# Sixteen expert blocks' first product computed during the key selection

## The reference, cut to what matters

```
q = (x @ w_q).reshape(tokens, 8 heads, 2, 128)
s1, s2 = q[:, :, 0] @ subkeys[0].T, q[:, :, 1] @ subkeys[1].T     # 128 keys each
v1, i1 = top_k(s1, 16); v2, i2 = top_k(s2, 16)
sc, pos = top_k(v1[..., :, None] + v2[..., None, :], 16)           # of 256 sums
eidx = i1 * 128 + i2 at pos                                        # 16384 experts
g = softmax(sc)
act = gelu(u_tab[eidx] . x)                                        # a dot product for each pick
out = sum over the 8 * 16 picks of g * act * v_tab[eidx]
```

## Time and profile before

| | us |
|---|---|
| median of 3 runs | 3969.11 |
| lowest, highest | 3940.86, 3989.34 |
| the profiled execution | 3945.24 |
| its span, first to last instruction | 3943.5 |

### The profile page before, as it was taken

One profiled execution on the slowest core, in us unless ns is written; L12 is line 12 of the kernel. 1 busy time (PEld: TensorE's weight loads), 2 busy tenths in 40 slices (PEclk: granted clock), 3 DMA queues, 4 the chain that ended last, 5 costly groups with the idle time before them and its releaser, 6 DMA issues. The chain is left out here.

```text
span 3943.5 us, 58724 instructions
## 1 busy us (share of the span) xinstructions
PE 3521.6 (89%) x19976; PEld 3186.6 (81%) x19996; DVE 3441.3 (87%) x7119; ACT 1494.6 (38%) x3188; POOL 1092.0 (28%) x1008
## 2 busy tenths in 40 slices
PE   4979989288999999999978999865799999999997
PEld 4957889277999999999977678864699999999996
DVE  8966759997999999999989565699799999999998
ACT  3322332283444334444333222314744344434433
POOL 0000123392333333333200001225633333333331
PEclk9978989599999999999988889887999999999998
DMA  6610110269999999999856001104699999999996
GB/s 243 234 60 24 54 45 23 81 207 352 414 407 401 402 401 402 405 400 400 338 183 221 23 1 54 66 1 160 218 387 411 404 402 396 410 402 403 404 403 245
DMA packets 199853, 1033.81 MB, mean 262 GB/s; under 512 B 18521, under 2 KB 70297, under 8 KB 95713
## 3 DMA queue, kind: packets, MB, share of 16 engines
q0 software_dynamic: 73728, 536.90, 33.4%
q1 hardware_dynamic: 125922, 494.56, 32.7%
HBM read 977.84 MB, written 53.56 MB: 262 GB/s over the span
## 5 line engine op out<-in xcount | busy, mean ns | idle before, releaser
L1592 POOL DMA_INDIRECT held_rows<-in_uv_rows,chosen x428 | 551.9, 1290 | 1489.2 <-DVE y L1911 1373.5
L1773 PE MATMUL ps<-hd_hi,u_hi 128*128 128x384 f32 x2048 | 701.0, 342 | 28.3 <-DVE a_lo L1890 18.5
L1773 PE MATMUL ps<-hd_hi,u_lo 128*128 128x384 f32 x2048 | 693.9, 339 | 0.0
L1773 PE MATMUL ps<-hd_lo,u_hi 128*128 128x384 f32 x2048 | 693.5, 339 | 0.0
L1911 DVE SCALAR_TENSOR_TENSOR y<-held_rows,shares_now,y 128x1024 f32<-128x1024 f32 x428 | 546.1, 1276 | 1.6 <-ACT shares_now L1830 1.6
L1901 DVE CUSTOM_DVE_ANT_0 held_rows<-held_rows,h2rows 128x1024 f32<-128x1024 f32 x428 | 520.2, 1215 | 0.4 <-DMA held_rows<-in_uv_rows,chosen 0.4
L1784 PE MATMUL ps<-v_hi,a_hi 128*128 128x512 f32 x1536 | 476.7, 392 | 0.0
L1784 PE MATMUL ps<-v_lo,a_hi 128*128 128x512 f32 x1536 | 472.8, 389 | 0.0
L1784 PE MATMUL ps<-v_hi,a_lo 128*128 128x512 f32 x1536 | 472.8, 389 | 0.0
L1815 ACT ACTIVATE v_hi<-v_raw 128x1024 fp32r<-128x1024 f32 x256 | 271.1, 1059 | 413.3 <-PE ps L1784 410.3
L1773 PEld LDWEIGHTS ps<-hd_hi,u_hi 128*128 128x128 f32 x2048 | 387.7, 189 | 39.0 <-DVE u_lo L1875 29.2
(11 more groups left out here) (308 smaller groups left out, 6926.5 us busy)
## 6 DMA issues: line engine op xcount, KB each, us to landing
u_raw<-in_u SPq DMA_DIRECT2D x128, 1024.0 KB, 13.6
v_raw<-in_v SPq DMA_DIRECT2D x128, 1024.0 KB, 9.0
mod_ring<-in_ada SPq DMA_DIRECT2D x96, 512.0 KB, 4.3
gates_dram<-gmat SPq DMA_DIRECT2D x12, 4096.0 KB, 13.8
gt<-gates_dram SPq DMA_DIRECT2D x64, 768.0 KB, 11.2
wq<-in_wq SPq DMA_DIRECT2D x8, 2048.0 KB, 7.6
w_odd<-in_w_in SPq DMA_DIRECT2D x8, 1024.0 KB, 5.2
w_even<-in_w_in SPq DMA_DIRECT2D x8, 1024.0 KB, 5.7
```

Source lines behind the costliest of these rows:

```text
L1592: pool.indirect_dma_start(picked(n).rearrange("p a d -> p (a d)"), None, a["uv_rows"], bass.IndirectOffsetOnAxis(ap=chosen[:, n % GT, n // ...
L1773: ins = pe.matmul(ps[:, b % 2, 0:TD], (u_hi, u_lo)[wl][:, b % 2, k, :], (hd_hi, hd_lo)[hl][:, k, :], start=(k == 0 and n == 0), stop=(k == ...
```

## The change

In `retrieve`, after the scores, PE computes `hidden` of the first 16 expert blocks of the layer. SP loads each u block into `ahead_raw`, ACT makes the high part, POOL the low part (`low_ahead`), ACT applies gelu from PSUM into `ahead_out`, and SP stores that to `ahead_dram`. There are two buffers of each. ACT's exp of the gates comes behind the gelu of block 8.

In `experts`, the first 16 blocks have no `hidden`, no gelu of it, and no split of u; SP loads the stored products, two blocks at a time, and `gate` multiplies from there into PSUM. The order of these blocks on ACT and DVE has the v block first. `hidden` of blocks 16 and 17 follows outputs 14 and 15.

The gathered rows are spread by `ROWS_OF`: one in each of the first 16 blocks, three in 16 of the other 112 (every seventh) and two in the other 96, 256 in all. ACT's gelu and share are done for each row alone.

```diff
+AHEAD_BLOCKS = 16
+AHEAD_BODIES = AHEAD_BLOCKS // BODY
+ROWS_OF = [1 if i < AHEAD_BLOCKS else 3 if i % 7 == 1 else 2 for i in range(NKEYS)]
...
+    ahead_dram = nc.dram_tensor("ahead_dram", [P, AHEAD_BLOCKS, TD], F32, kind="Internal").ap()
...
 # retrieve, sync
+                def store_ahead(b):
+                    sp.wait_ge(ahead_act, b + 1)
+                    sp.dma_start(ahead_dram[:, b, :], ahead_out[:, b % 2, :]).then_inc(ahead_stored[b % 2], 16)
+
+                sp.wait_ge(wq_split, 12)
+                for b in range(AHEAD_BLOCKS):
+                    if b >= 2:
+                        sp.wait_ge(ahead_split, b - 1)
+                    sp.dma_start(ahead_raw[:, b % 2, :, :], a["u"][l, b // 2][:, b % 2, :, :]).then_inc(ahead_in[b % 2], 16)
+                    if b >= 3:
+                        store_ahead(b - 3)
...
 # retrieve, tensor, after the scores
+                for b in range(AHEAD_BLOCKS):
+                    pe.wait_ge(ahead_split, b + 1)
+                    if b >= 2:
+                        pe.wait_ge(ahead_act, b - 1)
+                    for k in range(KD):
+                        for n, (wl, hl) in enumerate(PASSES):
+                            ins = pe.matmul(ps[:, b % 2, 0:TD], (ahead_hi, ahead_lo)[wl][:, b % 2, k, :],
+                                            (hd_hi, hd_lo)[hl][:, k, :], start=(k == 0 and n == 0), stop=(k == KD - 1 and n == 2))
+                    ins.then_inc(ahead_psum, 1)
...
 # retrieve, scalar
+                def high_ahead(b):
+                    act.wait_ge(ahead_in[b % 2], 16 * (b // 2 + 1))
+                    if b >= 2:
+                        act.wait_ge(ahead_psum, b - 1)
+                    act.activation(ahead_hi[:, b % 2, :, :], ahead_raw[:, b % 2, :, :], ACT.Copy).then_inc(ahead_high, 1)
+
+                def gelu_ahead(b):
+                    act.wait_ge(ahead_psum, b + 1)
+                    if b >= 2:
+                        act.wait_ge(ahead_stored[b % 2], 16 * (b // 2))
+                    act.activation(ahead_out[:, b % 2, :], ps[:, b % 2, 0:TD], ACT.Gelu_apprx_tanh).then_inc(ahead_act, 1)
...
-                act.wait_ge(gate_in, 1)
-                act.activation(best[:, :, :, :], best[:, :, :, :], ACT.Exp).then_inc(gate_exp, 1)
+                for b in range(AHEAD_BLOCKS):
+                    if b + 2 < AHEAD_BLOCKS:
+                        high_ahead(b + 2)
+                    gelu_ahead(b)
+                    if b == 8:
+                        act.wait_ge(gate_in, 1)
+                        act.activation(best[:, :, :, :], best[:, :, :, :], ACT.Exp).then_inc(gate_exp, 1)
...
 # retrieve, gpsimd
+                def low_ahead(b):
+                    pool.wait_ge(ahead_high, b + 1)
+                    pool.tensor_tensor(ahead_lo[:, b % 2, :, :], ahead_raw[:, b % 2, :, :], ahead_hi[:, b % 2, :, :],
+                                       ALU.subtract).then_inc(ahead_split, 1)
...
+                    if h == RH - 1:
+                        for b in range(3):
+                            low_ahead(b)
                     pool.wait_ge(sc_taken, 2 * h + 2)
...
+                for b in range(3, AHEAD_BLOCKS):
+                    low_ahead(b)
...
 # experts, sync
+                def load_ahead(j):
+                    if j >= 2:
+                        sp.wait_ge(gated, 2 * j - 2)
+                    at = 2 * j % 4
+                    sp.dma_start(ahead[:, at:at + 2, :], ahead_dram[:, 2 * j:2 * j + 2, :]).then_inc(ahead_back[j % 2], 16)
...
 # experts, tensor
-                hidden(0, 0)
-                hidden(0, 1)
-                body(0, first=True)
-                with pe.Fori(1, BODIES - 1) as i:
+                for i in range(AHEAD_BLOCKS):
+                    outputs(0, i, first=i == 0)
+                    if i >= AHEAD_BLOCKS - 2:
+                        hidden(0, i + 2)
+                with pe.Fori(AHEAD_BODIES, BODIES - 1) as i:
                     body(i)
...
 # experts, vector
+                for i in range(NKEYS):
+                    g, b = i // BODY, i % BODY
+                    before, now = (list(rows_of(i - 1)) if i >= 1 else []), list(rows_of(i))
+                    gate(g, b)
+                    if i < AHEAD_BLOCKS:
+                        low_v(g, b)
+                    for n in now[:-1]:
+                        dot(n)
+                    if AHEAD_BLOCKS <= i + 2 < NKEYS:
+                        low_u(g, b + 2)
+                    for n in before[:1]:
+                        weigh(n)
+                    low_a(g, b)
+                    for n in before[1:]:
+                        weigh(n)
+                    if i >= AHEAD_BLOCKS:
+                        low_v(g, b)
+                    dot(now[-1])
```

More of the change, by code:

```diff
@@ L1336, in build_program @@
     rows_back = K.sem("rows_back")
+    ahead_in = [K.sem(f"ahead_in{i}") for i in range(2)]
+    ahead_high = K.sem("ahead_high")
+    ahead_split = K.sem("ahead_split")
+    ahead_psum = K.sem("ahead_psum")
+    ahead_act = K.sem("ahead_act")
+    ahead_stored = [K.sem(f"ahead_stored{i}") for i in range(2)]
     def retrieve(l):
@@ L1707, in build_program @@
     dot_ready = K.sem("dot_ready")
+    ahead_back = [K.sem(f"ahead_back{i}") for i in range(2)]
     dot_act = K.sem("dot_act")
@@ L1718, in build_program, with rows_of @@
     ROWS_IN_ALL = GT * SLOTS
+    def rows_of(i):
+        at = sum(ROWS_OF[:i])
+        return range(at, at + ROWS_OF[i])
     def experts(l):
@@ L1751, in _ @@
                 for b in range(0, 4, 2):
+                    load_ahead(b // 2)
                     load_v(0, b)
                 load_g(0, 1)
-                with sp.Fori(0, BODIES - 1) as i:
+                for g in range(AHEAD_BODIES):
+                    body(g)
+                with sp.Fori(AHEAD_BODIES, BODIES - 1) as i:
                     body(i)
                 body(BODIES - 1, last=True)
-                sp.wait_ge(hid_psum, NKEYS + 2)
+                sp.wait_ge(hid_psum, NKEYS - AHEAD_BLOCKS + 2)
                 sp.dma_start(w_raw[0], a["w_first"][l]).then_inc(w_first, 16)
@@ L1833, in body @@
-                def body(g, last=False):
-                    for b in range(BODY):
-                        i = g * BODY + b
-                        act.wait_ge(hid_psum, g * BODY + b + 3)
-                        act.activation(ps[:, b % 2, 0:TD], ps[:, b % 2, 0:TD], ACT.Gelu_apprx_tanh).then_inc(hid_act, 1)
-                        if i >= 1:
-                            row_activations(i - 1)
-                        if not last or b < BODY - 2:
-                            high_u(g, b + 2)
-                        if i >= 1:
-                            row_shares(i - 1)
-                        act.wait_ge(gated, g * BODY + b + 1)
-                        act.wait_ge(out_psum, g * BODY + b + 1)
-                        act.activation(a_hi[:, b % 4, :], ps[:, b % 2, 0:TD], ACT.Copy).then_inc(a_high, 1)
-                        high_v(g, b)
@@ L1849, in _, with row_activation @@
-                high_u(0, 0)
-                high_u(0, 1)
-                for g in range(BODIES):
-                    body(g, last=g == BODIES - 1)
-                row_activations(SLOTS - 1)
-                row_shares(SLOTS - 1)
+                def row_activation(n):
+                    i, t = n // GT, n % GT
+                    act.wait_ge(dot_ready, n + 1)
+                    act.activation(acts[:, i % COLS, t:t + 1], dots[:, i % COLS, t:t + 1], ACT.Gelu_apprx_tanh).then_inc(dot_act, 1)
@@ new lines, in row_share, with high_a @@
+                def row_share(n):
+                    i, t = n // GT, n % GT
+                    act.wait_ge(dot_act, n + 1)
+                    if n >= COLS * GT:
+                        act.wait_ge(row_used, n - COLS * GT + 1)
+                    act.activation(shares_now[:, i % COLS, t:t + 1], acts[:, i % COLS, t:t + 1], ACT.Copy,
+                                   scale=gates[:, t, i:i + 1]).then_inc(share_ready, 1)
+                def high_a(g, b):
+                    act.wait_ge(gated, g * BODY + b + 1)
+                    act.wait_ge(out_psum, g * BODY + b + 1)
+                    act.activation(a_hi[:, b % 4, :], ps[:, b % 2, 0:TD], ACT.Copy).then_inc(a_high, 1)
@@ L1855, in _ @@
+                for n in rows_of(NKEYS - 1):
+                    row_activation(n)
+                    row_share(n)
                 for t in range(NT):
```

105 lines of the change are left out of this document (58 added, 47 removed).

## The result

The changed kernel took 4032.76 us (median of 4 runs, 3998.62 to 4059.14) against 3971.56 for the kernel before beside it (3940.86 to 3989.34). The ratio is 1.012, 95% interval 1.0061 to 1.0179: slower by 24 to 71 us. The ratio leaves out the slowest of the four executions, 4059.14, which ran in a slower state of the chip, so it is smaller than the ratio of the two medians. The profiled execution took 4028.68, its span is 4026.6.

What follows compares the result with a forecast made beforehand. PE was taken to set the pace, DVE having 4% to spare and DMA a third near-limit. Selection +24 and experts -30 gave -6 us a layer, -12 for two: 3957 us against the median 3969.1, range 3905 to 4015.

Steps and rivals of the forecast that it cites:

- The prediction's own sign of being wrong as a whole: Wrong if the expert stage gains less than 10 us, or the selection grows by less than 10 or more than 35.
- Key selection, +24 a layer: End of key selection: ten POOL subtractions of 2.43 us each hold up DVE's chain, +24 us, bounds +6 and +42.
- Rival (b): Key selection: POOL does not hold up DVE's bf16 chain, only +6 us; 3921, or 3881 if DMA keeps up; chance 0.17.
- (c): Key selection: POOL is starved and PE's chain ends last, +42, so +12 us a layer, 3993; chance 0.13.
- First 16 blocks, 4.8 each and 1.7 at the start: Experts: 4.8 us a block from DMA bytes, bounds 4.5 and 4.9; the first `outputs` starts 1.7 us later.
- The other 112 blocks, 8.44: Experts: 3.503 MB a block at 415 GB/s takes 8.44 us, bounds 8.31 and 8.67.
- the sum: Per layer: experts -30 us and selection +24 give -6; for two layers -12 us.
- Rival (a): Experts: DMA is the bound and slower; 4011 at 404 GB/s, 4049 at 397; chance 0.25.

Runs made afterwards that it cites:

- low_memset: Changed kernel with POOL's 16 subtractions replaced by fills of a buffer nobody reads; best minus gsum to the keys took 42.2 us, against 64.1.
- dve_low: Changed kernel with two rows in every block and DVE doing subtractions 7 to 15 itself; best minus gsum to keys 51.3 us, experts 1033.2 and 1031.3.
- dot_half: Changed kernel with dot products over 512 of 1024 columns, same bytes; the 112 blocks took 8.38 us each, against 8.60 to 8.66.
- spread_half: Changed kernel with eight rows moved instead of 16, three-row blocks at odd numbers; 8.29 and 8.27 us a block, first gate to last 1014.5 and 1012.2.
- dve_low_half: Changed kernel with DVE doing subtractions 7 to 15 and eight rows moved, on odd blocks; 3942.89 us against 3982.55 for the kernel before, ratio 0.9926.
- ulater_even: Eight rows moved, three-row blocks at even numbers, with u issued later than in that kernel; 8.28 and 8.30 us a block, against 8.45 and 8.43.
- ulater_12: Changed kernel with DVE doing subtractions 7 to 15, twelve rows moved on odd blocks, u issued later; 3960.39 us against 3985.14 before, ratio 0.996.

## Why the prediction was wrong, step by step

It gave 3957 us, 3905 to 4015, which is 12 us less than before and called no change. The median is 4032.8, outside the range; the kernel is slower, clear of the noise, though by less than 2%. The prediction's own sign of being wrong as a whole also came: the expert stage gained less than 10 us a layer (7 from first gate to last).

- **Key selection, +24 a layer: right**, +23.3, and by the mechanism named. The closeness is in part luck: eleven subtractions, not ten, fell beside DVE's chain, and each cost 2.1 us, not 2.43. The two-input products took 18.47 us for 11.85. Rival (b), no lock for bf16, is refuted; low_memset and dve_low show the cause. PE's chain did not end last, since PE waited 14.86 us for the keys, which refutes (c); and in dve_low, with all of PE's 16 products kept, the keys come 13 us earlier.
- **First 16 blocks, 4.8 each and 1.7 at the start: right in the number, not in the reason.** The mean is 4.83 to 4.91. The prediction took it from the bytes at 404 to 420 GB/s; 378 moved, most blocks took 4.41 us by DVE's own work (under its lower bound of 4.5), and a few late v blocks made up the rest. Keys to first gate grew by 1.7 us, which it did not have.
- **The other 112 blocks, 8.44: this step failed.** The prediction said: "I take 8.44 (415 GB/s), nearest to the best slice because the dips of now are time in which nothing was asked for, with some waits left in." Measured 8.60 to 8.66, mean 8.64: 23 us a layer, 45 in all, most of the 51 by which the stages missed the sum (39 measured, -12 forecast). It took one number for the stage, an average bandwidth, and its own two other numbers were not brought together with it: DVE at 58.1 of 58.1, and 10 waits for u that passed without harm because DVE had time. Over PE's pace of 8.31, which it also had, the blocks lost 0.37 us. Two things made it up. The transfers come in bunches of 2 MB: 0.17 us a block, shown by the moved wait. (That behind a three-row block the ring of six rows leaves a row one block's lead where it had two, and that this is what the bunch hits, is argued from the ring's length; no run changed the ring.) And DVE without slack turns late data into a stop of PE: the other 0.20 us. That DVE's slack counts is shown by dot_half, which takes away most of the whole loss with the same bytes; that it is all of the 0.20 is argued.
- **Rival (a)** was the nearest in time, 4011 at 404 GB/s and 4049 at 397. Its own figures at 404 GB/s, 8.67 a block and +21 a layer, are what was measured (+20). Its reason, the DMA engines at their ceiling, does not hold: with the same bytes they moved 413 GB/s in dot_half. There, with DVE's load halved in the dots, a block took 8.38, or 8.43 by PE's starts. So 8.44 is about what this stage takes with room on DVE, and the step lacked a term for DVE without room. I gave it 0.25 and let its price at 404, 4011, nearly close the range, over a base that lay 24 us above the profiled execution.
- **The whole-run figures** are 22 us further apart than the stages (medians 61, stages 39), from the mixer, below. With the step at its measured size the forecast would have been 4002, inside the range: of the 76 us by which it missed, the step explains 45, the other stages 6, the mixer 22, and the median before, which moved up by 2 with a fourth execution, the rest.

## What to carry to other kernels

An idle engine is not free: an operation with SBUF inputs on POOL beside a DVE chain costs DVE nearly its whole length (2.1 to 2.2 us of 2.4), so a piece that DVE itself does in half that time belongs on DVE, even where DVE sets the end. Balancing a stage until every engine is exactly full removes what absorbed the late transfers; moving half as much gained 29 us a layer here over moving all of it. Price such a step by the slack that is left in each block, not by an average. When loads of different streams are issued from one queue, look at when they leave: with 2 MB issued at one point DVE waited for its data and PE stopped (17 us a layer with eight three-row blocks on even numbers); with the same bytes issued 5 us apart it did not.

## What the runs showed of the hardware

- Which operations exclude each other on DVE and POOL depends on both. A POOL fill ran beside two-input bf16 operations of DVE at full speed on both sides, 0.96 us and 0.74 each; each of three subtractions beside them cost them 2.2 us (18.47 for 11.85). Beside the bf16 tensor_scalar, the fill alone waited and made DVE wait. The Trainium skill (SBUF — State Buffer, Who interferes with whom) states both: a two-input DVE instruction contends only with a GpSimd instruction that reads SBUF, one in a 2-port mode with any. These traces agree with the first; they fit the second if the tensor_scalar ran in such a mode, which no run here shows.
- The DMA engines moved 412 to 414 GB/s as a mean of 750 us in four kernels (spread_half, dot_half, dve_low_half, ulater_even). The 358 of the Trainium skill (DMA: Bandwidth & Descriptors, Specifications), which the prediction set against the trace, is 13% under that; the Trainium skill (HBM Reference, Specifications (TRN2)) takes it as the share of a core whose neighbour streams too, and gives about 425 for a core alone. The program runs on one core, and the measurement agrees with the second.
- The mixer ahead of each selection took 545 to 593 us in layer 1 and 518 to 566 in layer 2 over twenty profiles, with the same instructions. The time goes with the granted clock. Layer 1 from 300 to 450 us, the kernel before (549.6) and the changed one (581.1):

```profile
300.00:450.00 150.00, 143.86 (x887) 115.62 (x892) 102.75 (x281) 37.73 (x102) 0.00 (x0) 0.90 0.04 15
```

```profile
300.00:450.00 150.00, 145.34 (x690) 117.50 (x696) 78.09 (x213) 27.55 (x76) 0.00 (x0) 0.66 0.04 15
```

The granted clock is the column before the last two; its two levels are 0.5 (1.2 GHz) and 1.0 (2.4 GHz), and a stretch shows their mean. At 0.66 PE got through 690 matmuls where it did 887 at 0.90.

> The kernel before once more, for the spread of a stage that the change doesn't touch: the mixer part of the first layer took 549.6 us in the kernel before and 545 to 590 in the kernels with the change, with PE's granted clock low at another place each time. If that is chance, this run gives any value in 545 to 590, the other stages (160.8, 40.8, 160.0, 1049) within 2 us, and the ratios of whole runs carry that noise of some 20 us. If the change brings it about, it is near 550 again.

That run gave 546.8 and 550.2: layer 2 was 29 us over the first profile's 520.9, so the spread is there without the change. But layer 1 took 545 to 593, mean 575, in the 18 profiles with the change and 547 to 550 in two profiles of the one before; whether the change makes the slow clock there more frequent is open. It would explain why the whole-run ratios of dve_low_half and ulater_12 come out some 15 us less good than their stages.
